# Triangular inverses kept as four 32-row diagonal blocks instead of two 64-row blocks

## The chip, the cores and the metric

The kernel runs on one core of a Trainium2 chip. The metric is the device time of one launch in microseconds (us). The engines are TensorE (PE in the profile, its weight loads PEld), VectorE (DVE), ScalarE (ACT), GpSimd (POOL) and SyncE (SP, which issues the large loads).

## The reference

Two model blocks are computed after each other; the change touches the gated delta rule of the first. Cut to what matters:

```python
DN_HEADS, DN_HEAD_DIM, DN_CHUNK, N_META, SEQ = 4, 128, 64, 16, 256

def gated_delta_rule_chunked(q, k, v, beta, g):
    """S_t = exp(g_t)(I - beta_t k_t k_t^T) S_{t-1} + beta_t k_t v_t^T ; o_t = S_t^T q_t."""
    ...
    a = jnp.where(strict, jnp.einsum("bhnid,bhnjd->bhnij", k_beta, k) * lmask, 0.0)
    m = a + jnp.eye(c, dtype=a.dtype)
    u = lax.linalg.triangular_solve(m, v_beta, left_side=True, lower=True, unit_diagonal=True)
    w = lax.linalg.triangular_solve(m, k_beta * jnp.exp(decay)[..., None], left_side=True, lower=True,
                                    unit_diagonal=True)
    ...
```

All is in float32. The kernel does not use chunks of 64 but of 128 tokens, and one for the 16 meta tokens, so it solves with unit triangular matrices of 128 by 128: 4 heads times 2 chunks make 8 of them, and the four meta matrices lie together in a ninth.

## The kernel before, in words

The work is written out by hand: each engine has its own list of instructions, and semaphores order them. Nothing is planned by a scheduler, so an engine meets its waits in the order of the code.

The inverses are built by doubling. A level `lv` joins diagonal blocks of `1 << lv` rows into blocks of twice as many, in four steps. PE multiplies the matrix `AT` with the inverse so far `XIc` ("ax", L853). DVE masks the product out of PSUM into `TMc` (L2111). PE multiplies the masked product with the inverse and with its transpose `XITc`, into the banks "row" (L860) and "xax" (L864). DVE subtracts both from `XIc` (L2119) and `XITc` (L2120), and the next level's "ax" waits for that (`inv_step`). The nine matrices go through this in three parts (`PARTS`): matrices 0 to 3, 4 to 7, and the meta matrix, which needs only four levels. So PE and DVE work on one part while the other engine has the other.

Up to the sixth level (`INNER` = 6) only two diagonal blocks of 64 rows are kept for each matrix, 64 columns wide, and every product is one matmul for each block (`for rs in HALF_ROWS`), on a 64x64 tile of PE's array. The seventh level joins the two blocks of 64 (L870, L2124, L875, L2127) and writes the last quarter of the full inverse `XIT`; ACT copies the two diagonal blocks into `XIT` meanwhile (L1635), and POOL has cleared `XIT` long before (L623). Then PE waits for `chunk_act` and `inv_step` and starts the recurrence over chunks at L892. A float32 matmul of the code stands in the trace as two MATMUL and two LDWEIGHTS records: L853 is called 104 times and has 208 of each.

What runs beside the inverses: two loads that SP issued before (L532), three parameter broadcasts of POOL (L591), and the core's own instruction fetches, which the profile lists as a DMA queue of kind "instruction".

Of the kernel before, what the change touches and what calls it, by code (L numbers as in the profile page):

```python
# [17 lines left out]
P = 128  # L18
# [33 lines left out]
LEVELS = 7  # L52
# [9 lines left out]

SQUARES = ["ident", "upper", "strict", "ones", "lower", "mupper", "mones", "mlower"] + ["neg", "iota", "rep"]
VECTORS = ["emb_g", "emb_b", "mix0", "mix1", "mlp0", "mlp1", "ln2_g", "ln2_b", "ln1_g", "ln1_b"]
HALVES = ["eye2"] + [f"level{i}" for i in range(LEVELS - 1)]
SMALL = {"hmask": DN_H, "idx4": NG, "desc4": NG, "desc8": NE, "freq": HALF, "eps5": 1, "eps5a": 1, "eps6": 1, "one": 1, "zero": 1}


def const_layout():
    at, out = 0, {}  # L70
    for n, w in [("ident", P)] + list(SMALL.items()) + [(n, P) for n in SQUARES[1:]] + [(n, P // 2) for n in HALVES]:
        out[n] = (at, w)
        at += w
    return out, at


def shape_constants():
    lay, width = const_layout()
    c = np.zeros((P, width), np.float32)
    r, q = np.arange(P)[:, None], np.arange(P)[None, :]  # L80
    same = (r // 32 == q // 32) & (r % 32 < META) & (q % 32 < META)
    put = {
        "ident": r == q, "upper": r <= q, "strict": r < q, "ones": r >= 0, "lower": r >= q,
        "mupper": same & (r <= q), "mones": r // 32 == q // 32, "mlower": same & (r >= q),
        "neg": np.where(q <= r, 0.0, NEG), "iota": q + 0 * r,
        "rep": (q % 32 == r) & (r < META),
        "hmask": (r // 32 == np.arange(DN_H)[None, :]) & (r % 32 < META),
        "idx4": np.arange(NG)[None, :] + 0 * r, "desc4": NG - np.arange(NG)[None, :] + 0 * r,
        "desc8": NE - np.arange(NE)[None, :] + 0 * r,
        "freq": (np.float32(THETA) ** (-np.arange(0, ROT, 2, dtype=np.float32) / np.float32(ROT)))[None, :] + 0 * r,  # L90
        "eps5": LN_EPS + 0 * r, "eps5a": LN_EPS / ALPHA ** 2 + 0 * r, "eps6": RMS_EPS + 0 * r, "one": 1 + 0 * r, "zero": 0 * r,
    }
# [12 lines left out]
    for g, w in enumerate(WINDOWS):
        full = np.where((s <= t) & (s > t - w), np.float32(1) / np.minimum(t + 1, w).astype(np.float32), 0) - (s == t)
        bands[:, g, 0], bands[:, g, 1], bands[:, g, 2] = full[:P, :P], full[P:, P:], full[:P, P:]
    return c, bands.astype(np.float32)


def build(nc, t):
# [98 lines left out]
    QKT = cube(reg(8 * P), 8)  # L210
    kTm, vTm = reg(P), reg(P)
    gB, bB = AT, XI
    HW = P // 2
    HALF_ROWS = slice(0, HW), slice(HW, P)
    XIc, XITc = [cube(XI.rearrange("p c i -> p (c i)")[:, a * NM * HW:(a + 1) * NM * HW], NM) for a in range(2)]
    TMc = cube(TM.rearrange("p c i -> p (c i)")[:, 0:NM * HW], NM)
    vnew, state = AT[:, 0:4, :], XI[:, 0:4, :]
    rhs, odec = TM[:, 0:4, :], (LM[:, 4:8, :], LB[:, 0:4, :])
    junk = LB[:, 4:8, :]
# [276 lines left out]

        return C(name).unsqueeze(1).broadcast_to([P, n, P])

    def halves(name, n):

        return C(name).unsqueeze(1).broadcast_to([P, n, HW])

    INNER = LEVELS - 1
    META_LEVELS = 4

    def level_parts(lv):
# [6 lines left out]

    def with_rows(lv, i):

        return lv < INNER if i < 2 else lv < META_LEVELS - 1

    FIRST_HALF, SECOND_HALF = slice(0, D // 2), slice(D // 2, D)
    OUT_PARTS = [(0, slice(0, D)), (1, FIRST_HALF), (1, SECOND_HALF)]

    AX_BANK = B[0], B[1], B[6][:, 0:HW]
    ROW_BANK = B[2], B[3], B[6][:, HW:2 * HW]
    XAX_BANK = B[4], B[5], B[6][:, 2 * HW:3 * HW]

    @block.sync
    def _(sp):
# [62 lines left out]
    def _(pool):  # L589
# [54 lines left out]
    def _(pe):  # L644
# [198 lines left out]

        pe.wait_ge(S("chunk_dve"), 8)
        pe.wait_ge(S("chunk_act"), 3)
        for lv in range(INNER):
            for i, part in enumerate(level_parts(lv)):
                if lv:
                    pe.wait_ge(S("inv_step"), inverse_count(lv - 1, i))
                for j, c in enumerate(range(part.start, part.stop)):  # L850
                    for rs in HALF_ROWS:
                        ax = AX_BANK[i][rs, j * HW:(j + 1) * HW]
                        last = mm(ax, AT[rs, c, rs], XIc[rs, c, :], start=True, stop=True) if lv else mm(ax, AT[rs, c, rs], C("ident")[rs, rs], start=True, stop=True)  # L853
                last.then_inc(S("inv_ax"), 1)
            for i, part in enumerate(level_parts(lv)):
                pe.wait_ge(S("inv_masked"), inverse_count(lv, i))
                if lv and with_rows(lv, i):
                    for j, c in enumerate(range(part.start, part.stop)):
                        for rs in HALF_ROWS:
                            mm(ROW_BANK[i][rs, j * HW:(j + 1) * HW], XITc[rs, c, :], TMc[rs, c, :], start=True, stop=True)  # L860
                for j, c in enumerate(range(part.start, part.stop)):
                    for rs in HALF_ROWS:
                        xax = XAX_BANK[i][rs, j * HW:(j + 1) * HW]
                        last = mm(xax, TMc[rs, c, :], XITc[rs, c, :], start=True, stop=True) if lv else mm(xax, TMc[rs, c, :], C("ident")[rs, rs], start=True, stop=True)  # L864
                last.then_inc(S("inv_xax"), 1)
        upper_, lower_ = HALF_ROWS
        for i in range(NT):
            pe.wait_ge(S("inv_step"), inverse_count(INNER - 1, i))
            for j, c in enumerate(range(4 * i, 4 * i + 4)):
                last = mm(AX_BANK[i][lower_, j * HW:(j + 1) * HW], AT[upper_, c, lower_], XIc[upper_, c, :], start=True, stop=True)  # L870
            last.then_inc(S("inv_ax"), 1)
        for i in range(NT):
            pe.wait_ge(S("inv_masked"), inverse_count(INNER, i))
            for j, c in enumerate(range(4 * i, 4 * i + 4)):
                last = mm(XAX_BANK[i][upper_, j * HW:(j + 1) * HW], TMc[lower_, c, :], XITc[lower_, c, :], start=True, stop=True)  # L875
            last.then_inc(S("inv_xax"), 1)

        keep_going(2, 7, P)
# [644 lines left out]
    def _(sc):  # L1523
# [105 lines left out]
        sc.wait_ge(S("chunk_dve"), 3)  # L1629
        act(vb[:, 8, :], B[5][:, P:2 * P], ACT.Copy, scale=BE[:, 8:9]).then_inc(S("chunk_act"), 1)  # L1630
        sc.wait_ge(S("stacked"), 2)
        for i, ready in ((2, inverse_count(META_LEVELS - 1, 2)), (0, inverse_count(INNER - 1, 0)), (1, inverse_count(INNER - 1, 1))):
            sc.wait_ge(S("inv_step"), ready)
            for rs in HALF_ROWS:
# [307 lines left out]
    def _(dve):  # L1942
# [161 lines left out]
        line(last)  # L2104

        dve.wait_ge(S("stacked"), 2)
        for lv in range(INNER):
            for i, part in enumerate(level_parts(lv)):
                n = part.stop - part.start
                dve.wait_ge(S("inv_ax"), inverse_count(lv, i))  # L2110
                tt(TMc[:, part, :], cube(AX_BANK[i][:, 0:n * HW], n), halves(f"level{lv}", n), ALU.mult).then_inc(S("inv_masked"), 1)  # L2111
            for i, part in enumerate(level_parts(lv)):
                n = part.stop - part.start
                dve.wait_ge(S("inv_xax"), inverse_count(lv, i))
                dve.wait_ge(S("inv_masked"), inverse_count(lv, i))
                if lv:
                    dve.wait_ge(S("inv_step"), inverse_count(lv - 1, i))
                if with_rows(lv, i):
                    tt(XIc[:, part, :], XIc[:, part, :] if lv else halves("eye2", n), cube(ROW_BANK[i][:, 0:n * HW], n) if lv else TMc[:, part, :], ALU.subtract)  # L2119
                tt(XITc[:, part, :], XITc[:, part, :] if lv else halves("eye2", n), cube(XAX_BANK[i][:, 0:n * HW], n), ALU.subtract).then_inc(S("inv_step"), 1)  # L2120
        upper_, lower_ = HALF_ROWS
        for i in range(NT):
            dve.wait_ge(S("inv_ax"), inverse_count(INNER, i))
            nc.vector.tensor_copy(TMc[lower_, PARTS[i], :], cube(AX_BANK[i][lower_, 0:4 * HW], 4)).then_inc(S("inv_masked"), 1)  # L2124
        for i in range(NT):
            dve.wait_ge(S("inv_xax"), inverse_count(INNER, i))
# [600 lines left out]
```

## Time and profile before

| | us |
|---|---|
| median of 3 runs | 1021.08 (1020.49 to 1022.63) |
| the profiled execution | 1018.49 |
| its span in the profile | 1016.7 |
| from the first "ax" (129.30) to the wait's end at L892 (153.41) | 24.11 |
| PE, DVE, ACT busy over the whole span | 94%, 54%, 38% |

Times of rows count from the span's start. The span is 1.8 us shorter than the execution's own time. A busy PE is not PE at its peak: MATMUL records overlap, and their ends are modelled, so spacing is read from starts.

### The profile page before, as it was taken

The numbers are of one execution on the slowest core, as the hardware profiler recorded it, in microseconds if no ns is written. First come the engines' busy times: TensorE is split into PE (matmuls) and PEld (weight loads), VectorE is DVE, ScalarE is ACT, GpSimd is POOL, SyncE is SP. The second block draws the span as 40 slices with busy tenths as digits, with TensorE's granted clock in tenths as the row PEclk, the third lists the DMA queues.
The fourth block names the chain that finished last, engine by engine and source line by source line (L and its number), as shares of the span: only waits on it lengthen the run. The fifth ranks groups of instructions, "written<-read, shape, count | busy, mean of one in ns | idle before, by whom it ended". The sixth has DMA issues, their size and how long they took to land.

```text
span 1016.7 us, 15085 instructions
## 1 busy us (share of the span) xinstructions
PE 956.2 (94%) x6451; PEld 762.1 (75%) x6451; DVE 545.4 (54%) x821; ACT 386.9 (38%) x493; POOL 30.7 (3%) x49
## 2 busy tenths in 40 slices
PE   8999989999999987677899999999999999999997
PEld 7998886677776424242558888999999899999995
DVE  5884574996672121000077757565456685565464
ACT  4554503773252101000156454443343453433341
POOL 1400100003000000000000000000000000000000
PEclk9999999999999989879999999999999999999999
DMA  9824330446689999999996622455454444554421
GB/s 332 256 91 164 137 115 1 166 166 250 246 336 394 420 397 418 421 419 420 413 373 204 222 103 82 174 210 198 165 189 183 165 166 166 189 214 176 165 83 42
DMA packets 67276, 229.51 MB, mean 226 GB/s; under 512 B 4097, under 2 KB 5409, under 8 KB 54545
## 3 DMA queue, kind: packets, MB, share of 16 engines
q1 hardware_dynamic: 65360, 223.35, 57.8%
q0 software_dynamic: 1632, 5.26, 1.6%
q8 instruction: 43, 0.70, 0.3%
q14 instruction: 17, 0.13, 0.0%
q10 hardware_dynamic: 224, 0.07, 0.0%
HBM read 227.61 MB, written 1.05 MB: 225 GB/s over the span
## 4 chain that ended last, share of the span: by engine, by line
PE 81%; DMA 7%; DVE 7%; ACT 3%; issue 1%; SPq 0%; ACTq 0%; DVEq 0%
PE bank L1451 17%; PE bank L1462 16%; PE bank L1171 7%; PE bank L719 5%; DMA ring<-in_expert_w_up 4%; PE bank L1315 4%; PE bank L736 2%; PE bank L1041 2%; PE bank L1083 2%; PE bank L1377 2%; DMA X_xT<-in_expert_w_up 2%; PE bank L1319 2%; PE bank L1231 2%; PE bank L768 1%; PE bank L1208 1%; PE bank L1136 1%
## 5 line engine op out<-in xcount | busy, mean ns | idle before, releaser
L2519 DVE TENSOR_TENSOR w_lo<-ring,w_hi 128x2048 fp32r<-128x2048 f32 x76 | 170.6, 2288 | 86.2 <-ACT w_hi L1803 86.1
L1803 ACT ACTIVATE w_hi<-ring 128x2048 fp32r<-128x2048 f32 x76 | 141.2, 1910 | 92.4 <-PE bank L1462 86.7
L1451 PE MATMUL bank<-xT_hi,w_lo 128*128 128x256 f32 x480 | 136.0, 283 | 0.0
L1451 PE MATMUL bank<-xT_lo,w_hi 128*128 128x256 f32 x480 | 136.0, 283 | 0.0
L1451 PE MATMUL bank<-xT_hi,w_hi 128*128 128x256 f32 x480 | 135.9, 283 | 0.0
L1462 PE MATMUL bank<-w_hi,hidden_hi 128*128 128x512 f32 x256 | 99.9, 390 | 0.0
L1462 PE MATMUL bank<-w_lo,hidden_hi 128*128 128x512 f32 x256 | 99.9, 390 | 0.0
L1462 PE MATMUL bank<-w_hi,hidden_lo 128*128 128x512 f32 x256 | 99.7, 389 | 0.0
L1451 PEld LDWEIGHTS bank<-xT_hi,w_hi 128*128 128x128 f32 x480 | 92.2, 192 | 0.5
L1451 PEld LDWEIGHTS bank<-xT_lo,w_hi 128*128 128x128 f32 x480 | 92.2, 192 | 0.5
L1451 PEld LDWEIGHTS bank<-xT_hi,w_lo 128*128 128x128 f32 x480 | 92.2, 192 | 0.0
L1171 PE MATMUL bank<-arena 128*32 128x512 f32 x224 | 49.8, 659 | 16.4 <-DMA ring<-in_expert_w_up 11.9
L1900 ACT ACTIVATE arena<-bank 128x512 f32<-128x512 f32 x32 | 19.1, 598 | 114.4 <-PE bank L1451 110.6
L2411 DVE TENSOR_TENSOR X<-X,bank 128x256 f32<-128x256 f32 x9 | 3.8, 422 | 97.7 <-ACT X L1765 97.7
L2622 DVE TENSOR_TENSOR arena<-arena 128x512 f32<-128x512 f32 x32 | 22.1, 692 | 63.0 <-ACT arena L1900 62.8
L1462 PEld LDWEIGHTS bank<-w_hi,hidden_lo 128*128 128x128 f32 x256 | 48.1, 188 | 10.1
L1462 PEld LDWEIGHTS bank<-w_hi,hidden_hi 128*128 128x128 f32 x256 | 48.1, 188 | 9.7
L1462 PEld LDWEIGHTS bank<-w_lo,hidden_hi 128*128 128x128 f32 x256 | 48.1, 188 | 9.3
L1171 PE MATMUL bank<-ring,arena 128*32 128x512 f32 x192 | 43.6, 716 | 10.2 <-DMA ring<-in_expert_w_up 6.1
L1765 ACT ACTIVATE X<-bank 128x256 f32<-128x256 f32 x9 | 3.5, 383 | 108.5 <-PE bank L1171 102.1
L1171 PEld LDWEIGHTS bank<-arena 128*32 128x32 f32 x224 | 12.8, 120 | 39.3 <-issue 39.3
L2419 DVE COPY X<-bank 128x512 f32<-128x512 f32 x9 | 6.2, 691 | 61.5 <-PE bank L1208 54.1
(572 smaller groups left out, 1800.1 us busy)
## 6 DMA issues: line engine op xcount, KB each, us to landing
ring<-in_mlp_w_up SPq DMA_DIRECT2D x32, 1024.0 KB, 6.8
ring<-in_mlp_w_down SPq DMA_DIRECT2D x32, 1024.0 KB, 6.4
ring<-in_w_in SPq DMA_DIRECT2D x22, 1024.0 KB, 7.7
ring<-in_expert_w_down SPq DMA_DIRECT2D x20, 1024.0 KB, 12.8
arena<-in_expert_w_gate SPq DMA_DIRECT2D x14, 1024.0 KB, 12.9
arena<-in_expert_w_up SPq DMA_DIRECT2D x14, 1024.0 KB, 15.0
ring<-in_expert_w_gate SPq DMA_DIRECT2D x13, 1024.0 KB, 13.8
ring<-in_expert_w_up SPq DMA_DIRECT2D x13, 1024.0 KB, 16.0
```

What stands on the lines that cost most here:

```text
L719: last = mm(B[n % 4][:, 0:L], w_[:, k * 512 + c * P:k * 512 + (c + 1) * P], x_[:, k, IN_0:IN_W], start=(p_ == 0 and k == 0), stop=(p_ == 2 ...
L736: last = mm(B[n % 4][0:r, :], x_[:, k, IN_0 + a:IN_0 + a + r], w_[:, k * 512:(k + 1) * 512], start=(p_ == 0 and k == 0), stop=(p_ == 2 and ...
L1041: last = mm(B[n], x_(2 * part + kk, i), w_[:, kk * D + half * 512:kk * D + (half + 1) * 512], start=(part == 0 and p_ == 0 and kk == 0), s ...
L1083: last = mm(B[2 * (u - 13) + i], x_, w_, start=(part == 0 and p_ == 0 and kk == 0), stop=(part == 1 and p_ == 2 and kk == 3))
L1171: last = mm(cube(B[4][CAP * e:CAP * (e + 1), :], 2), xs[:, k, (q % 2) * P + CAP * e:(q % 2) * P + CAP * (e + 1)], w_[e][:, :, k, :], start ...
L1231: last = mm(B[2 * i + half], hTs[:, (2 + i) * P:(3 + i) * P], ysb[:, half * 512:(half + 1) * 512], start=first, stop=final)
L1315: mm(bank, x_[:, k, i * P:(i + 1) * P], w_hi[:, k * 512:(k + 1) * 512], start=(k == 0 and x_ is xTH), stop=False)
L1451: last = mm(B[4 + (2 * j + pr) % 4][:, cc * SEQ:(cc + 1) * SEQ], w_[:, k * 512 + c * P:k * 512 + (c + 1) * P], x_[:, k, 0:SEQ], start=(k = ...
L1462: last = mm(B[n], h_[:, j % 2, c, i * P:(i + 1) * P], w_[:, c * D + half * 512:c * D + (half + 1) * 512], start=(first and c == 0 and p_ = ...
L1803: act(whi[:, n % 2, half], slot(u)[:, half], ACT.Copy).then_inc(S("split_hi"), 1)
L2519: tt(wlo[:, u % SLOTS, half], slot(u)[:, half], f32(whi[:, n % 2, half]), ALU.subtract).then_inc(S("split_lo"), 1)
L2622: tt(r_, r_, r_, ALU.mult).then_inc(S("square_steps"), 1)
```

## The change

Up to the fifth level (`SMALL_LEVELS` = 5) four diagonal blocks of 32 rows are kept for each matrix, 32 columns wide, and every product is one matmul for each block (`for rs in QUARTER_ROWS`), on a 32x32 tile. The sixth level is written like the seventh: an "ax" of the off-diagonal block alone, a plain copy, and an "xax" that gives the off-diagonal block with its sign turned. It writes into `XIT` and into a new half-width inverse `XIh`, which the seventh level reads. ACT copies the blocks of 32 into both, so the seventh level waits for ACT (`chunk_act`) as well; POOL clears `XIh` too. The masks are 32 columns wide.

```diff
-HALVES = ["eye2"] + [f"level{i}" for i in range(LEVELS - 1)]
+SMALL_LEVELS = 5
+QUARTERS = ["eye4"] + [f"level{i}" for i in range(SMALL_LEVELS)]
...
-    XIc, XITc = [cube(XI.rearrange("p c i -> p (c i)")[:, a * NM * HW:(a + 1) * NM * HW], NM) for a in range(2)]
-    TMc = cube(TM.rearrange("p c i -> p (c i)")[:, 0:NM * HW], NM)
+    QUARTER_ROWS = [slice(QW * b, QW * (b + 1)) for b in range(4)]
+    XIc, XITc = [cube(XI_flat[:, a * NM * QW:(a + 1) * NM * QW], NM) for a in range(2)]
+    TMc = cube(TM_flat[:, 0:NM * QW], NM)
+    XIh, TMh = cube(XI_flat[:, 2 * NM * QW:2 * NM * QW + 8 * HW], 8), cube(TM_flat[:, 2 * NM * QW:2 * NM * QW + 8 * HW], 8)
...
+        nc.gpsimd.memset(XIh[:, :, :], 0.0)
         nc.gpsimd.memset(XIT[:, :, :], 0.0).then_inc(S("stacked"), 1)
...
-        for lv in range(INNER):
+        for lv in range(SMALL_LEVELS):
...
-                    for rs in HALF_ROWS:
-                        ax = AX_BANK[i][rs, j * HW:(j + 1) * HW]
+                    for rs in QUARTER_ROWS:
+                        ax = AX_BANK[i][rs, j * QW:(j + 1) * QW]
...
+        for i in range(NT):
+            pe.wait_ge(S("inv_step"), inverse_count(SMALL_LEVELS - 1, i))
+            for j, c in enumerate(range(4 * i, 4 * i + 4)):
+                for u_, l_ in (QUARTER_ROWS[0:2], QUARTER_ROWS[2:4]):
+                    last = mm(AX_BANK[i][l_, j * QW:(j + 1) * QW], AT[u_, c, l_], XIc[u_, c, :], start=True, stop=True)
+            last.then_inc(S("inv_ax"), 1)
+        for i in range(NT):
+            pe.wait_ge(S("inv_masked"), inverse_count(SMALL_LEVELS, i))
+            for j, c in enumerate(range(4 * i, 4 * i + 4)):
+                at = slice(j * QW, (j + 1) * QW)
+                for u_, l_ in (QUARTER_ROWS[0:2], QUARTER_ROWS[2:4]):
+                    last = mm(XAX_BANK[i][u_, at], TMc[l_, c, :], XITc[l_, c, :], start=True, stop=True)
+                l_ = QUARTER_ROWS[1]
+                last = mm(ROW_BANK[i][l_, at], XITc[l_, c, :], TMc[l_, c, :], start=True, stop=True)
+            last.then_inc(S("inv_xax"), 1)
         upper_, lower_ = HALF_ROWS
         for i in range(NT):
-            pe.wait_ge(S("inv_step"), inverse_count(INNER - 1, i))
+            pe.wait_ge(S("chunk_act"), 5 + i)
+            pe.wait_ge(S("inv_step"), inverse_count(SMALL_LEVELS, i))
...
-            for rs in HALF_ROWS:
+            for rs in QUARTER_ROWS[0:2] if i < 2 else ():
+                act(XIh[rs, PARTS[i], rs], XIc[rs, PARTS[i], :], ACT.Copy)
+            for rs in reversed(QUARTER_ROWS):
                 last = act(XIT[rs, PARTS[i], rs], XITc[rs, PARTS[i], :], ACT.Copy)
             last.then_inc(S("chunk_act"), 1)
...
-                tt(TMc[:, part, :], cube(AX_BANK[i][:, 0:n * HW], n), halves(f"level{lv}", n), ALU.mult).then_inc(S("inv_masked"), 1)
+                tt(TMc[:, part, :], cube(AX_BANK[i][:, 0:n * QW], n), quarters(f"level{lv}", n), ALU.mult).then_inc(S("inv_masked"), 1)
...
+        for i in range(NT):
+            dve.wait_ge(S("inv_ax"), inverse_count(SMALL_LEVELS, i))
+            nc.vector.tensor_copy(TMc[:, PARTS[i], :], cube(AX_BANK[i][:, 0:4 * QW], 4)).then_inc(S("inv_masked"), 1)
+        for i in range(NT):
+            dve.wait_ge(S("inv_xax"), inverse_count(SMALL_LEVELS, i))
+            l_ = QUARTER_ROWS[1]
+            ts(XIh[l_, PARTS[i], QUARTER_ROWS[0]], cube(ROW_BANK[i][l_, 0:4 * QW], 4), -1.0, None, ALU.mult)
+            for u_, l_ in (QUARTER_ROWS[0:2], QUARTER_ROWS[2:4]):
+                last = ts(XIT[u_, PARTS[i], l_], cube(XAX_BANK[i][u_, 0:4 * QW], 4), -1.0, None, ALU.mult)
+            last.then_inc(S("inv_step"), 1)
```

On PE, the second level (`lv` = 1) of the matrices 0 to 7 stands so before; "x7" is a row of seven like calls, and "bank0" and "bank1" take the "ax" products, "bank2" to "bank5" the "row" and "xax" products:

```order
L853 MATMUL bank0<-arena 64x64 [waits inv_step]
L853 MATMUL bank0<-arena 64x64 x7
L853 MATMUL bank1<-arena 64x64 [waits inv_step]
L853 MATMUL bank1<-arena 64x64 x7
...
L860 MATMUL bank2<-arena 64x64 [waits inv_masked]
L860 MATMUL bank2<-arena 64x64 x7
L864 MATMUL bank4<-arena 64x64 x8
```

and so in the change:

```order
L857 MATMUL bank0<-arena 32x32 [waits inv_step]
L857 MATMUL bank0<-arena 32x32 x15
L857 MATMUL bank1<-arena 32x32 [waits inv_step]
L857 MATMUL bank1<-arena 32x32 x15
...
L864 MATMUL bank2<-arena 32x32 [waits inv_masked]
L864 MATMUL bank2<-arena 32x32 x15
L868 MATMUL bank4<-arena 32x32 x16
```

The waits stand at the same places; behind each there are twice as many matmuls. On ACT the copies into `XIT` stand so before, the meta matrix first, then matrices 0 to 3 and 4 to 7:

```order
L1635 ACTIVATE arena<-arena 64x64 [waits inv_step,stacked]
L1635 ACTIVATE arena<-arena 64x64
L1635 ACTIVATE arena<-arena 64x4x64 [waits inv_step]
L1635 ACTIVATE arena<-arena 64x4x64
L1635 ACTIVATE arena<-arena 64x4x64 [waits inv_step]
L1635 ACTIVATE arena<-arena 64x4x64
```

and so in the change (L1655 writes `XIh`, L1657 `XIT`):

```order
L1657 ACTIVATE arena<-arena 32x32 [waits inv_step,stacked]
L1657 ACTIVATE arena<-arena 32x32 x3
L1655 ACTIVATE arena<-arena 32x4x32 [waits inv_step]
L1655 ACTIVATE arena<-arena 32x4x32
L1657 ACTIVATE arena<-arena 32x4x32 x4
L1655 ACTIVATE arena<-arena 32x4x32 [waits inv_step]
L1655 ACTIVATE arena<-arena 32x4x32
L1657 ACTIVATE arena<-arena 32x4x32 x4
```

Six copies now stand behind each of the two later waits, where two stood.

## Rows read from the trace of the kernel before

**Rows 1.** The page: busy time, share of the span, records.
```profile
PE 956.2 (94%) x6451; PEld 762.1 (75%) x6451; DVE 545.4 (54%) x821; ACT 386.9 (38%) x493; POOL 30.7 (3%) x49
```

**Rows 2.** Stretches: length, busy (records) by engine, granted clock, DMA share, GB/s.
```profile
129.30:153.41 24.11, 21.86 (x620) 20.50 (x621) 17.79 (x53) 2.17 (x6) 0.00 (x0) 1.00 0.24 94
129.30:132.50 3.20, 2.53 (x72) 2.25 (x72) 2.84 (x8) 0.00 (x0) 0.00 (x0) 1.00 1.04 426
135.86:139.84 3.98, 3.37 (x115) 3.36 (x113) 2.66 (x9) 0.00 (x0) 0.00 (x0) 1.00 0.01 4
146.68:150.08 3.40, 3.15 (x100) 2.95 (x97) 2.27 (x6) 0.02 (x1) 0.00 (x0) 1.00 0.02 5
```

**Rows 3.** Chain that ended last, 146.5 to 151.2: start, length, what.
```profile
147.22 0.34 DVE arena L2120
147.57 0.04 issue
147.61 0.68 PE bank L853 x16
148.29 0.47 PE bank L860 x16
148.76 0.47 PE bank L864 x16
149.23 0.47 PE bank L860 x16
149.69 0.49 PE bank L864 x16
150.21 0.42 DVE arena L2119
150.63 0.34 DVE arena L2120
```

**Rows 4.** Groups by form, 129.2 to 153.45: count, busy, mean ns, idle before.
```profile
L2111 DVE TENSOR_TENSOR arena<-bank,cst 128x256 f32<-128x256 f32 x12 | 5.0, 421 | 1.8 <-PE bank L853 1.8
L2111 DVE TENSOR_TENSOR arena<-bank,cst 128x64 f32<-128x64 f32 x4 | 0.9, 216 | 0.0
L1635 ACT ACTIVATE arena<-arena 64x256 f32<-64x256 f32 x4 | 1.7, 414 | 5.3 <-DVE arena L2120 5.2
L1635 ACT ACTIVATE arena<-arena 64x64 f32<-64x64 f32 x2 | 0.5, 255 | 17.9 <-DVE arena L2120 17.8
```

**Rows 5.** Chain that ended last, whole span: 128 MATMUL records on four 128x32 tiles.
```profile
101.04 3.63 PE bank L748 x128
```

**Rows 6.** Timeline, 136.6 to 137.3: start, length, engine, count, idle before.
```profile
136.71 0.13 PEld L853 LDWEIGHTS bank<-arena 64*64 64x64 f32 x1 [0.29 <-DVE arena L2120]
137.16 0.33 PE L853 MATMUL bank<-arena 64*64 64x64 f32 x5 [0.61 <-DVE arena L2120]
137.16 0.25 PEld L853 LDWEIGHTS bank<-arena 64*64 64x64 f32 x6 [0.33 <-issue]
```

**Rows 7.** DMA, 134.4 to 136.0, in 40 slices; queue: packets, MB, share of 16 engines.
```profile
GB/s 154 205 154 205 154 51 717 51 0 0 0 0 0 0 51 0 51 0 51 0 51 0 51 0 51 0 51 0 0 0 0 0 0 0 0 0 0 0 0 0
q8 instruction: 1, 0.02, 4.3%
```

**Rows 8.** DMA, 137 to 154, in 40 slices of 0.425 us.
```profile
GB/s 0 0 0 39 0 0 0 0 0 0 0 39 0 0 0 0 0 0 0 0 0 39 0 0 0 0 0 0 0 0 39 0 0 0 0 0 0 0 0 0
q8 instruction: 4, 0.07, 1.5%
```

**Rows 9.** DMA, 20 to 330: instruction queue; and PE's records in that stretch.
```profile
q8 instruction: 20, 0.33, 0.4%
20.00:330.00 310.00, 299.98 (x2446) 242.47 (x2445) 205.43 (x390) 143.16 (x213) 25.07 (x35) 1.00 0.53 196
```

**Rows 10.** Timeline of POOL, 115 to 118.
```profile
116.09 1.06 POOL L623 MEMSET arena<- 128x1152 f32 x1 [8.04 <-PE bank L811]
```

**Rows 11.** Chain that ended last, 126 to 156: the seventh level and its end.
```profile
151.01 0.69 PE bank L870 x8
152.88 0.64 PE bank L649 x4
```

More of the change, by code:

```diff
@@ L70, in const_layout @@
     at, out = 0, {}
-    for n, w in [("ident", P)] + list(SMALL.items()) + [(n, P) for n in SQUARES[1:]] + [(n, P // 2) for n in HALVES]:
+    for n, w in [("ident", P)] + list(SMALL.items()) + [(n, P) for n in SQUARES[1:]] + [(n, P // 4) for n in QUARTERS]:
         out[n] = (at, w)
@@ L92, in shape_constants @@
     }
-    row = r % (P // 2)
-    put["eye2"] = row == q
-    for i in range(LEVELS - 1):
+    row = r % (P // 4)
+    put["eye4"] = row == q
+    for i in range(SMALL_LEVELS):
         s = 1 << i
@@ L212, in build @@
     gB, bB = AT, XI
-    HW = P // 2
+    HW, QW = P // 2, P // 4
     HALF_ROWS = slice(0, HW), slice(HW, P)
-    XIc, XITc = [cube(XI.rearrange("p c i -> p (c i)")[:, a * NM * HW:(a + 1) * NM * HW], NM) for a in range(2)]
-    TMc = cube(TM.rearrange("p c i -> p (c i)")[:, 0:NM * HW], NM)
+    QUARTER_ROWS = [slice(QW * b, QW * (b + 1)) for b in range(4)]
+    XI_flat, TM_flat = XI.rearrange("p c i -> p (c i)"), TM.rearrange("p c i -> p (c i)")
+    XIc, XITc = [cube(XI_flat[:, a * NM * QW:(a + 1) * NM * QW], NM) for a in range(2)]
+    TMc = cube(TM_flat[:, 0:NM * QW], NM)
+    XIh, TMh = cube(XI_flat[:, 2 * NM * QW:2 * NM * QW + 8 * HW], 8), cube(TM_flat[:, 2 * NM * QW:2 * NM * QW + 8 * HW], 8)
     vnew, state = AT[:, 0:4, :], XI[:, 0:4, :]
@@ L497, in masks, with quarters @@
         return C(name).unsqueeze(1).broadcast_to([P, n, P])
-    def halves(name, n):
-        return C(name).unsqueeze(1).broadcast_to([P, n, HW])
-    INNER = LEVELS - 1
+    def quarters(name, n):
+        return C(name).unsqueeze(1).broadcast_to([P, n, QW])
     META_LEVELS = 4
@@ L514, in with_rows @@
     def with_rows(lv, i):
-        return lv < INNER if i < 2 else lv < META_LEVELS - 1
+        return i < 2 or lv < META_LEVELS - 1
     FIRST_HALF, SECOND_HALF = slice(0, D // 2), slice(D // 2, D)
     OUT_PARTS = [(0, slice(0, D)), (1, FIRST_HALF), (1, SECOND_HALF)]
-    AX_BANK = B[0], B[1], B[6][:, 0:HW]
-    ROW_BANK = B[2], B[3], B[6][:, HW:2 * HW]
-    XAX_BANK = B[4], B[5], B[6][:, 2 * HW:3 * HW]
+    AX_BANK = B[0], B[1], B[6][:, 0:QW]
+    ROW_BANK = B[2], B[3], B[6][:, QW:2 * QW]
+    XAX_BANK = B[4], B[5], B[6][:, 2 * QW:3 * QW]
     @block.sync
@@ L858, in _ @@
                     for j, c in enumerate(range(part.start, part.stop)):
-                        for rs in HALF_ROWS:
-                            mm(ROW_BANK[i][rs, j * HW:(j + 1) * HW], XITc[rs, c, :], TMc[rs, c, :], start=True, stop=True)
+                        for rs in QUARTER_ROWS:
+                            mm(ROW_BANK[i][rs, j * QW:(j + 1) * QW], XITc[rs, c, :], TMc[rs, c, :], start=True, stop=True)
                 for j, c in enumerate(range(part.start, part.stop)):
-                    for rs in HALF_ROWS:
-                        xax = XAX_BANK[i][rs, j * HW:(j + 1) * HW]
+                    for rs in QUARTER_ROWS:
+                        xax = XAX_BANK[i][rs, j * QW:(j + 1) * QW]
@@ L866, in _ @@
         upper_, lower_ = HALF_ROWS
         for i in range(NT):
-            pe.wait_ge(S("inv_step"), inverse_count(INNER - 1, i))
+            pe.wait_ge(S("chunk_act"), 5 + i)
+            pe.wait_ge(S("inv_step"), inverse_count(SMALL_LEVELS, i))
             for j, c in enumerate(range(4 * i, 4 * i + 4)):
-                last = mm(AX_BANK[i][lower_, j * HW:(j + 1) * HW], AT[upper_, c, lower_], XIc[upper_, c, :], start=True, stop=True)
+                last = mm(AX_BANK[i][lower_, j * HW:(j + 1) * HW], AT[upper_, c, lower_], XIh[upper_, c, :], start=True, stop=True)
@@ L871, in _ @@
             last.then_inc(S("inv_ax"), 1)
         for i in range(NT):
-            pe.wait_ge(S("inv_masked"), inverse_count(INNER, i))
+            pe.wait_ge(S("inv_masked"), inverse_count(SMALL_LEVELS + 1, i))
             for j, c in enumerate(range(4 * i, 4 * i + 4)):
-                last = mm(XAX_BANK[i][upper_, j * HW:(j + 1) * HW], TMc[lower_, c, :], XITc[lower_, c, :], start=True, stop=True)
+                last = mm(XAX_BANK[i][upper_, j * HW:(j + 1) * HW], TMh[lower_, c, :], XIT[lower_, c, lower_], start=True, stop=True)
@@ L1631, in _ @@
         sc.wait_ge(S("stacked"), 2)
-        for i, ready in ((2, inverse_count(META_LEVELS - 1, 2)), (0, inverse_count(INNER - 1, 0)), (1, inverse_count(INNER - 1, 1))):
+        for i, ready in ((2, inverse_count(META_LEVELS - 1, 2)), (0, inverse_count(SMALL_LEVELS - 1, 0)), (1, inverse_count(SMALL_LEVELS - 1, 1))):
             sc.wait_ge(S("inv_step"), ready)
-            for rs in HALF_ROWS:
+            for rs in QUARTER_ROWS[0:2] if i < 2 else ():
+                act(XIh[rs, PARTS[i], rs], XIc[rs, PARTS[i], :], ACT.Copy)
+            for rs in reversed(QUARTER_ROWS):
                 last = act(XIT[rs, PARTS[i], rs], XITc[rs, PARTS[i], :], ACT.Copy)
@@ L2106, in _ @@
         dve.wait_ge(S("stacked"), 2)
-        for lv in range(INNER):
+        for lv in range(SMALL_LEVELS):
             for i, part in enumerate(level_parts(lv)):
@@ L2118, in _ @@
                 if with_rows(lv, i):
-                    tt(XIc[:, part, :], XIc[:, part, :] if lv else halves("eye2", n), cube(ROW_BANK[i][:, 0:n * HW], n) if lv else TMc[:, part, :], ALU.subtract)
-                tt(XITc[:, part, :], XITc[:, part, :] if lv else halves("eye2", n), cube(XAX_BANK[i][:, 0:n * HW], n), ALU.subtract).then_inc(S("inv_step"), 1)
+                    tt(XIc[:, part, :], XIc[:, part, :] if lv else quarters("eye4", n), cube(ROW_BANK[i][:, 0:n * QW], n) if lv else TMc[:, part, :], ALU.subtract)
+                tt(XITc[:, part, :], XITc[:, part, :] if lv else quarters("eye4", n), cube(XAX_BANK[i][:, 0:n * QW], n), ALU.subtract).then_inc(S("inv_step"), 1)
+        for i in range(NT):
[8 more added lines that the diff above has]
+            last.then_inc(S("inv_step"), 1)
         upper_, lower_ = HALF_ROWS
         for i in range(NT):
-            dve.wait_ge(S("inv_ax"), inverse_count(INNER, i))
-            nc.vector.tensor_copy(TMc[lower_, PARTS[i], :], cube(AX_BANK[i][lower_, 0:4 * HW], 4)).then_inc(S("inv_masked"), 1)
+            dve.wait_ge(S("inv_ax"), inverse_count(SMALL_LEVELS + 1, i))
+            nc.vector.tensor_copy(TMh[lower_, PARTS[i], :], cube(AX_BANK[i][lower_, 0:4 * HW], 4)).then_inc(S("inv_masked"), 1)
         for i in range(NT):
-            dve.wait_ge(S("inv_xax"), inverse_count(INNER, i))
+            dve.wait_ge(S("inv_xax"), inverse_count(SMALL_LEVELS + 1, i))
             ts(XIT[upper_, PARTS[i], lower_], cube(XAX_BANK[i][upper_, 0:4 * HW], 4), -1.0, None, ALU.mult).then_inc(S("inv_step"), 1)
```

## The prediction, made before the changed kernel ran

> **What bounds the kernel now.** I began with the page: TensorE (PE) is busy 94% of the span [rows 1], an average over stages with different limits, so what counts is the stretch that the change touches. It runs from the first "ax" at 129.30 to the end of the wait at L892 at 153.41, 24.11 us [rows 2]. The chain that ended last runs through it without a break: "ax", row and xax matmuls, the two subtractions of DVE, and the next "ax" [rows 3]. So a microsecond gained or lost here is one of the kernel. One level without the meta matrix takes 3.40 us; PE is busy 3.15 of it and DVE 2.27 [rows 2]. The granted clock is 1.00, the upper level, throughout.
>
> Two things set a level's length. The first is PE's own work: 16 MATMUL records of one group take 0.47 us [rows 3], 29 ns each; two 64x64 tiles work in turn, so one tile takes 58.5 ns for 64 columns. The second is latency: a group's last result comes 0.68 − 0.47 = 0.21 us late, and DVE's operations stand between PE's groups.
>
> A third thing shows once. At 136.71 PE has loaded a weight and its MATMUL starts only at 137.16, with six more loads behind it, and the 0.33 us ahead of these is put down to "issue", to no semaphore [rows 6]. In that stretch the instruction queue moves a packet, whose bytes show at 134.64 as a slice of 717 GB/s; it lasts 4.3% x 16 x 1.6 = 1.10 us, to 135.75 [rows 7]. PE goes on 1.4 us later. From 20 to 330 us this queue has 20 packets, 0.33 MB, so 16.5 KB each, while PE has 2446 + 2445 records: 245 records to a packet [rows 9]. I read this as blocks of 256 PE instructions of 64 bytes, and the pause as PE at the end of a block, waiting for the next one. The next packet starts at 137 + 3 x 0.425 = 138.3, that is 1.15 us after PE went on [rows 6, 8]: a block appears to be ordered only when the one ahead of it is begun.
>
> **The change part by part.**
>
> *Matmuls.* Four blocks for each matrix instead of two double the calls of the levels that remain. A call is four records (two MATMUL, two weight loads). Before, the stage has 308 calls, 1232 records, which the 620 + 621 of the view confirm [rows 2]. After, the levels have 72, 108, 108, 104 and 96 calls, the new sixth level 40 and the last 16: 544 calls, 2176 records. The cost in the array of one on a 32x32 tile isn't in the trace. The nearest row is L748: 128 records on four 128x32 tiles in 3.63 us, 28 ns each, so about 113 ns for 128 columns on one tile [rows 5]. 58.5 ns for 64 columns and 113 for 128 give a straight line with 31 ns for 32 columns: 7.8 ns a record with four tiles at work. The bounds are 58.5/8 = 7.3 ns and 58.5/4 = 14.6 ns (no gain from the shorter stream). I take 8.3, a little above the line: a group of 32 records then takes 0.27 us instead of 0.47.
>
> *DVE.* 128x256 takes 421 ns and 128x64 takes 216 [rows 4]; on a line between them 128x128 takes 284. A second subtraction starts 0.34 behind the first now [rows 3]; I take 0.20.
>
> *The sixth level.* It loses the mask and becomes a copy and three sign changes, each in 128 elements or less a row. That is no more DVE work than in a small level. ACT has six copies behind each of its two later waits instead of two. A copy of 64x256 takes 414 ns and one of 64x64 takes 255 [rows 4]; on the line between, 128 elements take about 0.32: 12 copies, 3.9 us. They are hidden today under the seventh level; now the seventh level's "ax" waits for them, so at least the last six, 1.9 us, lie on the path. POOL's additional clearing is less than half of its 128x1152 memset of 1.06 us, done by 117.2 [rows 10], twelve microseconds before it is needed: nothing. Fewer and narrower mask constants change one load by little: nothing.
>
> *Half-chain if only this counted.* A part goes through "ax" 0.27, its late result 0.25 (0.21 and 0.04 of issue), mask 0.28, 0.06 to PE, row and xax 0.53, late result 0.25, subtractions 0.20 + 0.28, 0.06 to PE: 2.2 us a level instead of 3.40. Both parts hold PE for 6 x 0.27 = 1.6, less than that. Five levels: 10.9.
>
> *The supply of instructions.* The five levels' 1952 records in 10.9 us would use up a block of 256 every 1.4 us. A round of ordering and getting one is, from above, 1.15 us to the packet, 1.0 for the packet (four packets in 17 us, 1.5% x 16 x 17 / 4 = 1.02 [rows 8]), and 1.4 from its end until PE goes on: 3.5 us. Before, 100 + 97 records a level of 3.40 us [rows 2] use up a block in 4.4 us, so the supply is just ahead; packets in 137 to 154 start 3.4 to 4.3 us apart (slices 3, 11, 21, 30 of 0.425 [rows 8]). I know of no stretch of before where blocks come faster: L748 itself, 128 MATMULs and their loads, uses one in 3.63 us [rows 5].
>
> So I count from the block ends. PE's stream ahead of the stage is unchanged. The pause at 136.71 is the second block end of the stage before, about record 393 by counting calls; every further one is 256 on: 649, 905, 1161, 1417, 1673, 1929 of 2176. The block behind record 393 comes at about the same time as before, since it waits for its packet among the loads (the DMA share up to 132.50 is 1.04 [rows 2]): between 135.8, where its packet ended, and 137.2, say 136.3. Six rounds of 3.5 follow, 21.0: the one behind record 1929, just ahead of the end of the fifth level, is there at 157.3. Then come its last 23 records (0.2), late result and subtractions (0.25 + 0.54), six copies of ACT (1.9), and the seventh level with its end, which takes from 151.01 to 153.41 now, 2.40 [rows 2, 11], with 0.2 of waits: 5.5 us, bounds 5 and 7. The end of the wait moves to 162.8 instead of 153.4: **+9.4 us**. Behind L892 nothing changes, and other engines wait for it.
>
> [...]
>
> **The rivals.**
>
> *The supply hides (faster).* If blocks lie ready further ahead than I think, latency decides: 10.9 us for five levels and some 0.6 at the first, where the mask waits for DVE's earlier work, then the sixth level's and ACT's copies and the end, 3.9 + 2.4. That is 17.8 against 24.1: −6.3, 1014.8 us. For it: only one pause is plain in the trace, and it fell while the loads were running; the share of DMA falls to 0.01 behind it [rows 2]. Against it: the packets behind it still start one by one, as PE uses them up [rows 8].
>
> *The round is shorter (no change).* If the 1.4 us behind the packet belong to that one pause and not to the supply, a round is 2.15 us. Then 134.4 + 6 x 2.15 + 5.5 = 152.8 against 153.4: nothing that can be measured. A round of about 2.0 to 2.5 us is where the change of sign lies.
>
> [...] No row here has 32 columns.
>
> *The array at its upper bound (no change).* At 14.6 ns a group of 32 takes 0.47 as before, a level about 3.2, and only the dropped row and xax products of the sixth level are gained while ACT's copies are added: about −1 us. The supply at 3.5 us a round would be slower than this, so it decides only where that fails.
>
> *PE issues no faster (slower).* Every row in PE's busiest stretches has a MATMUL each 28 or 29 ns [rows 3, 5]. If that is the floor of issue and not the array, a full level of 192 MATMULs takes 4.8 to 5.6 us (25 to 29 ns): five levels 24 to 28, end 6.3, against 24.1: +6 to +11. The sum is like mine; what tells them apart is even spacing instead of pauses.
>
> **How the numbers follow.** Supply 0.56, issue floor 0.16, a shorter round 0.06, the array at its upper bound 0.04, hidden supply 0.18. The likeliest gives 1021.1 + 9.4 = 1030.5 us as median; the profiled execution now is 1018.49, 1.8 above its span, so its span would be near 1026. The likeliest one's own range is 1028 to 1035 (rounds of 3.3 to 3.85 us, so 20 to 23; first block 135.8 to 137.2; end of 5 to 7). The range reaches from 1016.5, part of the way to the hidden supply, over no change, to 1037, which leaves out under 2 in 10. Slower by over 0.2% (2 us, about what a measurement can tell from nothing) 0.72, within it 0.10, faster 0.18.
>
> **What would show it.** Right: in the stage PE has pauses put down to "issue" of about 2 us, one every 256 records; eight or nine instruction packets stand there, 3.5 us apart; within a block MATMULs start about 8 ns apart; DVE's 128x128 takes near 0.28 us and ACT's copy 0.32. Wrong: packets closer than 2.5 us without pauses, or starts evenly 25 to 29 ns apart, or ACT's copies ahead of L890 longer than 1.9 us.

## The result and the profile after

The changed kernel takes 1039.7 us in the median of 4 runs (1039.19 to 1041.53) against 1021.67 of the kernel before: a ratio of 1.0181 (95% interval 1.0167 to 1.0195), 18.0 us slower. Forecast were +9.4 us, 1030.5, and at most 1037.0. The direction was right, and the cause forecast for it is there, but the loss is 8.6 us larger than forecast, and more than half of that excess lies behind the stage, where I had put nothing. The profiled execution is 1039.19 us long, its span 1037.0; that of before was 1018.49, low for its kernel, so spans differ by 20.3.

The page's busy line, beside [rows 1]:

```profile
PE 958.7 (92%) x6923; PEld 763.4 (74%) x6923; DVE 541.3 (52%) x823; ACT 389.5 (38%) x503; POOL 32.6 (3%) x50
```

PE has 6923 − 6451 = 472 MATMULs more, the 944 records of the forecast's 2176 − 1232 together with their loads, and is hardly busier: 958.7 against 956.2 us. Most of the loss is idle time. The chain that ended last, through the stage: its pauses and a few rows beside them, the rows between left out:

```profile
132.26 0.83 PE bank L857 x52
133.09 3.62 issue
136.71 0.48 PE bank L857 x16
137.24 0.37 PE bank L864 x28
138.64 1.53 issue
142.34 1.57 issue
145.84 1.81 issue
149.73 1.38 issue
153.38 1.19 issue
156.50 1.53 issue
161.06 1.89 PE bank L890 x15
163.06 1.63 PE bank L895 x15
164.69 1.15 PE bank L653 x4
165.84 0.43 PE bank L912 x2
```

Here the chain looked quite otherwise in [rows 3]: matmuls and subtractions without a break. Now it is cut by seven pauses that are put down to "issue". They end at 136.71, 140.17, 143.91, 147.65, 151.11, 154.57 and 158.03, so 3.46 to 3.74 us apart, and together they are 12.63 us long. In the stretch of the six rounds behind the first pause, 136.70 to 158.00 (the second of the windows below), PE has 768 MATMULs and 768 loads: 256 records a round, the size of block that the forecast had read from 245 records to a packet. The first pause stands behind 52 MATMULs of the second level: 288 records of the first level and 104 make 392, the block end 393 of the forecast. Between pauses 28 MATMULs take 0.37 us, 13 ns each. The DMA of 137 to 160, in 40 slices of 0.575 us, beside [rows 8]:

```profile
GB/s 0 28 0 0 0 0 0 28 0 0 0 0 0 28 0 0 0 0 0 0 28 0 0 0 0 0 28 0 0 0 0 0 28 0 0 0 0 0 28 0
q8 instruction: 7, 0.11, 2.0%
```

Seven instruction packets where 137 to 154 had four, one every 3.5 us. Read round by round, in slices of 0.09 us, one starts 1.0 to 1.15 us behind each pause's end, lasts 0.9 to 1.2 us (its share of the 16 engines times the round), and the next pause ends 1.3 to 1.5 us later: the three parts of the forecast's round (1.15, 1.0 and 1.4). The second thing that changed is the clock (stretch, length, busy PE, PEld, DVE, ACT, POOL, granted clock, DMA share, GB/s):

```profile
133.10:136.70 3.60, 0.00 (x0) 0.00 (x0) 0.00 (x0) 0.00 (x0) 0.00 (x0) 0.96 0.53 204
136.70:158.00 21.30, 12.28 (x768) 11.25 (x768) 6.12 (x29) 2.44 (x10) 0.00 (x0) 0.50 0.02 5
161.00:165.80 4.80, 4.74 (x37) 4.65 (x38) 2.49 (x7) 0.00 (x0) 0.00 (x0) 0.50 0.00 0
165.80:170.00 4.20, 4.20 (x24) 2.27 (x23) 0.00 (x0) 1.06 (x5) 0.00 (x0) 0.85 0.02 4
```

From 136.4, late in the first pause, to 167.1, behind the stage, PE's granted clock is 0.50; before, the stage had 1.00 throughout [rows 2]. 1.00 and 0.50 are the only two values in the traces here, the upper and the lower level below; one between them, as 0.96 or 0.85, is the mean of a stretch in which the clock changed. Between pauses that costs nothing, since the next block isn't there anyway: in a version below (the broadcasts held back) the first round ran at 1.00, and it took 3.46 us as others do at 0.50. It costs behind the last pause. The seventh level with its end, 161.06 to 165.84, takes 4.78 us; before, it began at 151.01 [rows 11] and L892 ran at 153.52: 2.51 us. At L912, once L892, the kernel is 165.84 − 153.52 = 12.3 us late.

The third place is far from the change. It stands behind the branch for spilled tokens, in the chain at 535 to 560:

```profile
535.95 0.87 PE bank L660 x6
536.82 3.63 issue
540.46 2.39 PE bank L660 x10
542.85 12.62 PE bank L1325 x48
555.46 3.63 PE bank L1335 x16
```

In before, the same work has no pause, and after ten of the 16 MATMULs of L656 (here L660) the chain goes on through ACT:

```profile
520.97 1.32 PE bank L656 x10
...
523.55 11.19 PE bank L1305 x48
534.74 3.63 PE bank L1315 x16
```

PE waits 3.63 us for nothing that the profile names, then the granted clock is at its lower level (0.50 from 540.4 to 546.0): ten MATMULs of L660 take 2.39 us, where ten of them took 1.32 before, and L1325 takes 12.62 instead of 11.19. From the start of L660 to that of L1335 it is 555.46 − 535.95 = 19.51 us, before 534.74 − 520.97 = 13.77: 5.7 us lost.

### The profile page after: what moved, and what is told of

It reads as the page before. It is cut to its first block, busy times and chain, and to the rows that moved or that the text cites. A ratio compares the mean times of both kernels' runs of the same rounds, so it can differ in the third digit from the quotient of the medians.

```text
span 1037.0 us, 16042 instructions
## 1 busy us (share of the span) xinstructions
PE 958.7 (92%) x6923; PEld 763.4 (74%) x6923; DVE 541.3 (52%) x823; ACT 389.5 (38%) x503; POOL 32.6 (3%) x50
## 4 chain that ended last, share of the span: by engine, by line
PE 80%; DMA 7%; DVE 7%; issue 3%; ACT 3%; SPq 0%; ACTq 0%; DVEq 0%
PE bank L1471 17%; PE bank L1482 16%; PE bank L1191 6%; PE bank L723 5%; DMA ring<-in_expert_w_up 4%; PE bank L1335 3%; PE bank L740 2%; PE bank L1061 2%; PE bank L1103 2%; PE bank L1397 2%; DMA X_xT<-in_expert_w_up 2%; PE bank L1339 2%; PE bank L1251 2%; PE bank L1228 2%; PE bank L772 1%
## 5 line engine op out<-in xcount | busy, mean ns | idle before, releaser
L1191 PE MATMUL bank<-arena 128*32 128x512 f32 x224 | 47.5, 645 | 17.3 <-DMA ring<-in_expert_w_up 11.4
L1191 PE MATMUL bank<-ring,arena 128*32 128x512 f32 x192 | 41.4, 696 | 11.5 <-DMA ring<-in_expert_w_up 7.2
```

The source lines that it names most:

```text
L1191: last = mm(cube(B[4][CAP * e:CAP * (e + 1), :], 2), xs[:, k, (q % 2) * P + CAP * e:(q % 2) * P + CAP * (e + 1)], w_[e][:, :, k, :], start ...
```

## The experiments

All are changes to one of the two kernels, and each time and its ratio stand beside runs of before from the same chip. A ratio isn't exactly that of the two medians (they are up to 1.6 us apart here), so both are given where it matters.

**Code that never runs.** The branch for spilled tokens isn't taken. Instructions put into it move what stands behind it, and nothing else:

```diff
         with pe.If(flag):
...
             pe.wait_ge(S("moe_out"), 4 * PASSES + 4)
+            keep_going(20, 7, 8)     # 80 records in the changed kernel; 44 (176) and 52 (208) in before
```

> The changed kernel with 20 calls (80 records of PE) put into the branch for spilled tokens, which is not taken: they never run, and only move the code behind the branch by 80 instructions, so that 944 + 80 = 1024 = 4 x 256 stand ahead of it more than before. Theory of block ends: the pause of 3.63 us in L660 (536.82) and the lower clock behind it go, some 5 to 6 us: about 1034 us instead of 1039.7. Rival, the later loss comes from the loads of the experts or from the clock alone: within 1 us of 1039.7. The stage of the inverses itself stays as it is, ending some 12.5 us later than before.

Measured: 1034.98 us (1033.73 to 1035.8), ratio 1.0122 (1.0105 to 1.0139), so 4.7 us are back by the medians, 6.0 by the ratios (1.0181 − 1.0122). L660 has no pause in its chain, and ten of its MATMULs take 1.33 us as before. The stage ends as in the change, but for 0.4 us (L912 at 166.25), since two of its rounds took 4.0 us (pauses end at 150.41, 154.43 and 158.44).

> The kernel before with 44 calls (176 records, as 944 is 176 above 3 x 256) in the branch that is not taken; nothing that runs is changed. Theory of block ends: a pause of 3 to 4 us appears inside L656 right behind the branch, the clock falls behind it, and the time is 4 to 6 us above before, some 1026 to 1027. Rival: code that doesn't run costs nothing, 1021 to 1022.

Measured: 1027.35 us (1027.21 to 1028.04), ratio 1.0054 (1.0037 to 1.007), 6.4 us above the median of 1020.98 beside it (5.5 by the ratio). The pause is where it was expected (timeline of PE: start, length, count, idle before):

```profile
524.42 0.98 PE L656 MATMUL bank<-cst,X 128*128 128x128 f32 x7 [0.75 <-DVE X L1975]
528.97 2.18 PE L656 MATMUL bank<-cst,X 128*128 128x128 f32 x9 [3.56 <-issue]
```

> As the version with 176 records in the branch that is not taken, which ran 6.4 us longer, but with 208: 32 records more that never run. There the pause of 3.56 us came 14 records into L656, with few instructions between the branch and L656. Theory of block ends: 32 more put the branch's target behind that block end, at the start of a block, so the pause goes: 1021 to 1022 us. Rival, a longer jump or more code costs time: as with 176 or more, 1027 and above.

Measured: 1020.97 us against 1021.27, ratio 1.0 (0.9989 to 1.0012). So 32 instructions more that never run take the loss away again: the time follows neither the amount of code nor the length of the jump. Where the branch's target lies in its block fits all three versions (80 records in the change: 4.7 us less; in before, 176: 6.4 us more, 208: nothing).

**The supply by itself.** A train of calls that wait for nothing, in the kernel before, between the seventh level and the recurrence:

```diff
+        for k in range(512):
+            rs = QUARTER_ROWS[k % 4]
+            at = 32 * (k % 16 // 4)
+            mm(B[7][rs, at:at + 32], ident[rs, rs], cst[rs, lay["upper"][0]:lay["upper"][0] + 32], start=True, stop=True)
         keep_going(2, 7, P)
```

> The kernel before with 512 more calls (2048 records, 8 blocks of 256) of 32x32 tiles with 32 columns between the seventh level and the recurrence, four tiles in turn, waiting for nothing. It measures the disputed cost by itself. Supply theory: a pause put down to issue at each block end, rounds of 3.5 us, 8 x 3.5 = 28 us, within a block 8 to 15 ns from MATMUL to MATMUL; with the lower clock behind it some 30 to 32 us more in all. Array theory: no pauses, 1024 x 8.3 ns = 8.5 us (15 us at 14.6 ns). Issue floor: evenly 25 to 29 ns, 26 to 30 us without pauses.

Measured, in the chain:

```profile
153.16 1.98 PE bank L883 x217
155.14 2.33 issue
157.47 1.66 PE bank L883 x90
159.13 2.07 issue
161.20 1.93 PE bank L883 x96
163.14 1.53 issue
```

Seven pauses in all, ending 3.46 to 3.74 us apart, as in the changed kernel; the train takes 26.4 us, to 179.53. The first 217 MATMULs take 9.1 ns each, at a granted clock of 1.00. By the forecast's counting (block ends 1417 and 1673 from the stage's start, the stage before has 1232 records) a block ends some 185 records into the train, and it passes without a pause: the instruction queue moved a packet at 150.3, done by 151.4, before the train began. The first pause stands where the second end is due, some 441 records in. From 159.13 on, at 0.50, the 128 MATMULs of a round take 1.93 us, 15 ns each.

> Control to the train of 32 columns: the same 512 calls on the same tiles with 128 columns, four times the stream. Supply theory: the array needs 1024 x 27 ns = 27.6 us, a block is used up in 3.5 us, about as fast as one comes: no pauses or ones under 0.3 us, clock at its upper level, 27 to 29 us between the seventh level and the recurrence, the same as the train of 32 columns took (26.4). Array theory: four times as long as the 32-column train's work.

With 128 instead of 32 in the four places above, the whole train is one row:

```profile
155.33 28.08 PE bank L883 x1024
```

Four times the stream takes 28.08 instead of 26.4 us, without a pause (27.4 ns a MATMUL), at a clock of 1.00. A block lasts 28.08 / 8 = 3.5 us there, and the supply keeps up. (Both trains ran once, and are read from their traces alone.) In the two trains it is the number of instructions in a time that decides, and not what one of them does.

**Fewer instructions in the changed kernel.**

```diff
-                    for rs in QUARTER_ROWS:
+                    for rs in QUARTER_ROWS[0:2]:
```

at the three products of the five small levels.

> The changed kernel with the products of the five small levels issued for two of the four 32-row blocks alone; the inverses of the other two blocks are left out (their rows hold stale numbers), all else runs as in the change. The stage has 1200 records instead of 2176, about as many as before (1232). Supply theory: only three rounds behind the first pause instead of six, 3 x 3.5 us = 10.5 us less, so the wait at the end of the stage near 151 to 154, and with fewer pauses less of the lower clock: about 1022 to 1025 us. Rival, 32x32 tiles or the chain of small DVE and ACT operations are slow by themselves: the stage stays longer than before by at least half of its 12.5 us.

Measured: 1022.14 us (1020.82 to 1023.29), ratio 1.0006 (0.9996 to 1.0015). One pause over 1 us is left:

```profile
136.15 1.36 issue
...
149.03 1.89 PE bank L890 x15
...
153.81 0.43 PE bank L912 x2
```

L912 is reached at 153.81, 12.0 us earlier than in the change and 0.3 later than before. This version has 32 records fewer than before, not 944 more, and the pause behind the branch is gone as well (5.7 us): ten MATMULs of L660 take 1.32 us, from 524.11. Together that is 17.7 us, and by the medians it is 17.6 us faster than the change. The pauses hang on the number of records, then, and with as many records as before the stage with small tiles and short DVE operations is no slower than before, though only half of the small products are computed. But there is no gain over before either. The seventh level with its end takes 4.78 us again (149.03 to 153.81), and the windows show a lower clock:

```profile
127.90:131.20 3.30, 1.79 (x46) 1.48 (x44) 2.89 (x6) 0.00 (x0) 0.00 (x0) 1.00 1.00 337
131.20:153.80 22.60, 20.04 (x569) 19.10 (x570) 12.17 (x52) 4.51 (x16) 0.00 (x0) 0.50 0.19 75
```

The clock fell at 131.2, ahead of any long pause, after PE had been busy for 1.79 of 3.30 us in the first level, where it waits for DVE. That alone doesn't tell why: in the same stretch the changed kernel's PE was busy for 1.83 us, and its clock stayed at 1.00 until 136.4, late in the first pause. Whether it would stay up with a faster supply was not tried.

**The first pause and the loads.** POOL's broadcasts are held back behind the inverses in the changed kernel:

```diff
         pool.wait_ge(S("proj"), GATE0)
+        pool.wait_ge(S("inv_step"), inverse_count(SMALL_LEVELS + 2))
```

> The changed kernel with POOL's three parameter broadcasts held back until the inverses are done (they are used at 190). Theory: the first pause, 3.62 us at 133.09, is long because the packet waits among the loads; with half of them gone its block comes 1 to 2 us earlier, all six rounds behind it too: the stage ends 1 to 2 us earlier, 1037.5 to 1038.7 us. Rival: the other loads alone fill the queues as well, no change, 1039.7.

Measured: 1037.1 us (1036.18 to 1038.98), ratio 1.0164 (1.0141 to 1.0186): 2.6 us less than the changed kernel by the medians of two sets, 1.7 by the ratios, whose intervals overlap. So the trace has to tell it. The pauses:

```profile
133.21 0.43 issue
134.99 2.11 issue
139.06 1.50 issue
...
153.16 1.81 issue
```

The block behind record 393 comes at 133.64 instead of 136.71, 3.07 us earlier, and the last pause ends at 154.97 instead of 158.03, 3.06 earlier: the rounds behind it are the same, as the theory has it. The size was larger than I expected: not half of the loads were gone but nearly all, the DMA share from 130.0 to 133.2 is 0.04, where the change has 1.06 from 131.2 to 133.1. Of the 3.07 us the profiled execution has 1.54 left at L660 (534.41 against 535.95), and the pause behind the branch is there as in the change (3.89 us).

**One part of the change alone.** The kernel before with the sixth level written as in the change:

```diff
-        for lv in range(INNER):
+        for lv in range(INNER - 1):
...
+                    last = mm(AX_BANK[i][l_, j * QW:(j + 1) * QW], AT[u_, c, l_], XIc[u_, c, 0:QW], start=True, stop=True)
...
+            ts(XIc[l_, PARTS[i], 0:QW], cube(ROW_BANK[i][l_, 0:4 * QW], 4), -1.0, None, ALU.mult)
+            for u_, l_ in (QUARTER_ROWS[0:2], QUARTER_ROWS[2:4]):
+                last = ts(XITc[u_, PARTS[i], QW:HW], cube(XAX_BANK[i][u_, 0:4 * QW], 4), -1.0, None, ALU.mult)
```

> The kernel before with only its sixth level done as in the change (off-diagonal blocks of 32 rows on 32x32 tiles, copy and sign change, written in place in the 64-column layout; no additional copies on ACT). 40 calls instead of 48. Theory: this part alone is a gain, the level's chain goes from 3.40 to about 2.4 us, no pause at a block end is added, and the kernel is 1 us faster (1020.6), too little for the timed runs but to be seen in the stage. Rival: more and smaller DVE operations eat it up, 0.

Measured: 1023.01 us (1021.42 to 1024.44), ratio 1.0022 (1.0009 to 1.0036): 2 us slower. The chain at its end:

```profile
150.12 0.50 PE bank L887 x5
...
151.31 1.11 PE bank L892 x8
152.43 1.15 PE bank L651 x4
153.57 0.43 PE bank L909 x2
154.00 1.71 PE bank L904 x2
```

The seventh level starts at 150.12 instead of 151.01, 0.9 earlier, as expected. But while DVE did its six sign changes one by one, PE was busy for only 2.12 of the 3.00 us from 147.9 to 150.9 (before, a level has 3.15 of 3.40 [rows 2]), and the granted clock is at its lower level, 0.50, from 150.9 to 157.7: keep_going takes 1.15 instead of 0.64 us, L904 1.71 instead of 0.86. Two versions against that: six empty calls on PE (keep_going(6, 7, P)) behind the sixth level's products, and the sign changes of the transposed inverse given to ACT.

> The sixth level done alone as in the change, and behind its products six calls of 128x128 that compute nothing, so that PE does not idle while DVE does its six sign changes. In the version without them the level ended 0.9 us earlier than before, but the clock fell at 150.9 and gave 1.8 us back. Theory: with PE busy the clock stays up, and the stage ends 0.5 to 0.9 us earlier than before. Rival: the clock falls all the same or the calls stand in the way, no gain over before.

Measured: 1021.41 us against 1021.2, ratio 1.0004 (0.9994 to 1.0013). The clock stays up in the stage (1.00 from 145 to 155), but the calls hold up the seventh level (its second half starts at 150.91, without them at 150.12), and the stage ends 0.3 us later than before: no gain, as the rival has it.

```diff
-            for u_, l_ in (QUARTER_ROWS[0:2], QUARTER_ROWS[2:4]):
-                last = ts(XITc[u_, PARTS[i], QW:HW], cube(XAX_BANK[i][u_, 0:4 * QW], 4), -1.0, None, ALU.mult)
...
+                for u_ in QUARTER_ROWS[0::2]:
+                    act(XITc[u_, PARTS[a], QW:HW], cube(XAX_BANK[a][u_, 0:4 * QW], 4), ACT.Copy, scale=-1.0).then_inc(S("chunk_act"), 1)
```

> The sixth level done alone as in the change, but the two sign changes into the transposed inverse are ACT's (idle then), DVE does one for each part; the seventh level's first product waits for DVE's one alone. Theory: the level's chain loses four times 0.30 us, PE's idle time at its end becomes short enough for the clock to stay up, the stage ends 1.5 to 2 us earlier than before: 1019 to 1019.5 us, at the bound of what the timing can tell. Rival: ACT's copies behind it become late for the recurrence's wait, no gain.

Measured: 1020.52 us against 1021.2, ratio 0.9996 (0.9984 to 1.0007).

```profile
151.20 0.64 PE bank L651 x4
151.84 0.37 PE bank L910 x2
```

In the profile the stage ends 153.52 − 151.84 = 1.7 us earlier with the clock up (1.00 from 145 to 155), as expected; the time expected (1019 to 1019.5) was not reached, and the timed runs do not tell this from nothing. The broadcasts held back as well (the line of the version above, with LEVELS):

> The version with the sixth level alone and ACT's sign changes (its stage ended 1.7 us earlier than before, 1020.5 us against 1021.2), and the broadcasts held back until the inverses are done. Theory: the pause of 0.45 us at 136.71 goes as well: the stage ends 2 to 2.5 us earlier than before, 1019 to 1020 us. Rival: the broadcasts, now at 153 to 166, come too late for their use or stand in the way of the next loads: 1021 or more.

Measured: 1020.42 us against 1021.27, ratio 1.0003 (0.9984 to 1.0022). The pause at 136.97 (0.24 us on the chain of the version above) is gone, but the profiled execution had the clock down at 0.50 from 151.0 to 154.4, and the stage ends at 152.26, 1.3 us earlier than before and not 2 to 2.5. No version here is shown to beat before.

## Why the prediction was right and wrong

**The supply of instructions: right, and shown.** Block ends by counting, a round of 3.5 us (3.46 to 3.74 here, up to 4.0 with 80 dead records), the first block at 136.3 (136.71), the one behind record 1929 at 157.3 (158.03). The trains show it alone, and with half of the small products the stage ends within 0.3 us of before. The rivals fall with it: the supply isn't hidden, and a round isn't 2.15 us. MATMULs in a block stand 9 ns apart at the upper clock and 13 to 15 at the lower, so PE's issue has no floor of 25 to 29 ns, and the array isn't at its upper bound of 14.6. (The 25 of that rival was an estimate that no run shows: rows of before stand 28 or 29 ns apart [rows 3, 5], and those of the train of 128 columns 27.4.)

A block's end is not hidden once blocks are used up faster than they come: seven ends here cost 12.63 us. But the next block is fetched while one runs: its packet starts 1.0 to 1.15 us behind the pause's end, while PE works on, and the train's first 217 MATMULs, 434 records with their loads, ran without a pause over a block end.

**The small durations: about right, one term by luck.** DVE's 128x128 takes 280 to 290 ns (forecast 284), ACT's copy 306 (forecast 320, where the line through the two rows gives 308). The copies were forecast to hold the seventh level up by 1.9 us. They hold up nothing: its first product (L890, 161.06) needs the copies of matrices 0 to 3, done at 158.31, and DVE's sign changes of them, done at 160.93. What stands on the path instead is the sixth level itself, 158.99 to 160.93, which the sum had left out. It happens to be 1.9 us long too. So it is luck that from the last pause's end to 161.06 it comes to 3.0 us, where I had 3.1.

**"The seventh level with its end, which takes from 151.01 to 153.41 now, 2.40": mis-sized.** It takes 4.78, at a granted clock of 0.50 that PE has had since 136.4, late in the first pause. At 0.50 a MATMUL of its first product lasts 311 ns instead of 219 (ends are modelled), and keep_going 1.15 us instead of 0.64; with half of the small products left out it is the same 4.78 at 0.50. I had the pauses and never asked what clock PE would have behind them. With the 0.5 us of the recurrence's first steps (12.3 us late at L912, 12.8 at L916, which starts at 167.60 and started at 154.76 before) this is 2.8 us of the miss.

**"Behind L892 nothing changes": the step that failed.** 944 instructions more, 176 above three blocks, move every block end behind the stage. Behind the branch at L1284 one fell some 12 records into work that the chain waits for, and the packet that PE then waits for moves only in the pause (the instruction queue has one at 531 and the next at 537): 5.7 us in the trace, 4.7 to 6.0 in the timed runs. I had counted block ends as far as the stage's end and no further. The three versions with code that never runs show that it is the block's end, and not the loads or the experts' work.

The account: 9.4 forecast, 0.7 in the supply, 2.3 + 0.5 by the clock, 4.7 behind the branch (by the medians), 17.6 of the 18.0 measured. With 5.7 or 6.0 there it would be 0.6 or 0.9 more than measured; the account closes to within 1 us, no better. The lower clock in L1228 at 521.85 (5.38 us, where the profiled execution of before has 3.69) is not the change's: before with 208 dead records has a stretch of lower clock at 509.5 to 512.9 and 5.38 us too, and its time is that of before.

## What to carry to other kernels

Cutting matmuls into smaller ones multiplies instructions, and a long row of them was supplied here at no more than 256 records in about 3.5 us, however small they were: divide the records of a stage by its time before dividing its columns. After any change in the number of instructions look behind the next branch for a pause that waits for "issue"; some instructions in a branch that isn't taken can move it away (80 records did here, 4.7 us). And where a pause of PE is forecast, cost the matmuls behind it at the lower clock: here the same end of the stage took 4.78 us at 0.50 and 2.51 at 1.00.

## What was not expected of the hardware

- Code that never runs changes the time: 176 records in a branch not taken cost 6.4 us (5.5 by the ratio), 208 cost nothing (1027.35 and 1020.97 us).
- An instruction block comes 3.1 us later while loads fill the DMA engines: the first was there at 136.71 (DMA share 1.06 ahead of the pause), and with POOL's broadcasts held back at 133.64 (share 0.04).
- The lower clock can come without a long pause of the supply: with half of the blocks left out it fell to 0.50 at 131.2, ahead of the pause at 136.15. Why it fell there, and only at 136.4 in the change, stays open.
